# Order of GpSimd's back substitution and of its decay transfers, and place of the decay exponentials on ScalarE, in a block of attention and gated DeltaNet

## The reference

```python
gcum = jnp.cumsum(g, axis=-1)
decay = jnp.exp(jnp.where(causal, gcum[..., :, None] - gcum[..., None, :], -jnp.inf))
a_mat = jnp.einsum('bnhid,bnhjd->bnhij', k_beta, k) * decay * strict
rhs = jnp.concatenate([v * beta[..., None], k_beta * jnp.exp(gcum)[..., None]], axis=-1)
sol = lax.linalg.triangular_solve(eye + a_mat, rhs, left_side=True, lower=True,
                                  unit_diagonal=True)
qk = jnp.einsum('bnhid,bnhjd->bnhij', q, k) * decay
```

## Time and profile before

| | |
|---|---|
| median of 3 runs | 1907.46 us (1907.27 to 1907.67) |
| the profiled execution | 1907.71 us, of which the span is 1905.9 us |
| TensorE busy | 1887.0 us, 99% of the span |
| VectorE busy | 1250.8 us, 66% |
| ScalarE busy | 1039.5 us, 55% |
| GpSimd busy | 105.6 us, 6% |
| granted TensorE clock | 0.998 |

### The profile page before, as it was taken

One profiled execution on the slowest core, in us unless ns is written; L12 is line 12 of the kernel. 1 busy time (PEld: TensorE's weight loads), 2 busy tenths in 40 slices (PEclk: granted clock), 3 DMA queues, 4 the chain that ended last, 5 costly groups with the idle time before them and its releaser, 6 DMA issues.

```text
span 1905.9 us, 27743 instructions
## 1 busy us (share of the span) xinstructions
PE 1887.0 (99%) x9497; PEld 1585.5 (83%) x9497; DVE 1250.8 (66%) x2189; ACT 1039.5 (55%) x2108; POOL 105.6 (6%) x208
## 2 busy tenths in 40 slices
PE   9999999999999999999999999999999999999997
PEld 8888888888888888888888788888888888888886
DVE  6658888898888665655666776555555555545555
ACT  4447776667767554555444655544444445444442
POOL 2001022111220100000000000000000000000000
PEclk9999999999999999999999999999999999999999
DMA  8666565555654657665565465556555555665552
GB/s 318 208 157 179 149 146 138 116 165 130 151 132 142 193 189 248 198 199 190 195 245 181 152 219 199 190 185 197 181 194 189 186 183 191 224 207 189 196 199 89
DMA packets 204180, 349.63 MB, mean 183 GB/s; under 512 B 6768, under 2 KB 73024, under 8 KB 203088
## 3 DMA queue, kind: packets, MB, share of 16 engines
q1 hardware_dynamic: 200704, 334.00, 52.7%
q0 software_dynamic: 3264, 14.47, 5.6%
q10 hardware_dynamic: 144, 0.26, 0.0%
HBM read 344.32 MB, written 2.10 MB: 182 GB/s over the span
## 4 chain that ended last, share of the span: by engine, by line
PE 83%; DVE 9%; issue 4%; POOL 2%; ACT 2%; DMA 1%; DVEq 1%; ACTq 0%; POOLq 0%; SPq 0%
PE dense L658 23%; PE dense L660 23%; PE dense L659 23%; PE dense L646 5%; PE dense L648 3%; DVE lo L1518 2%; DMA raw<-in_w_in_dram 1%; POOL less L571 1%; POOL sub L574 1%; PE chain L822 1%; PE chain L1104 1%; DVE pad L1689 0%; DVE qd L1814 0%; PE chain L924 0%; PE chain L916 0%
## 5 line engine op out<-in xcount | busy, mean ns | idle before, releaser
L1518 DVE TENSOR_TENSOR lo<-raw,hi 128x512 fp32r<-128x512 f32 x1252 | 843.0, 691 | 427.2 <-ACT hi L1154 423.8
L1154 ACT ACTIVATE hi<-raw 128x512 fp32r<-128x512 f32 x1252 | 777.0, 630 | 632.3 <-PE dense L660 611.5
L658 PE MATMUL dense<-hi,xs 128*128 128x512 f32 x1376 | 540.0, 392 | 1.8 <-DVE xs L2081 1.1
L660 PE MATMUL dense<-lo,xs 128*128 128x512 f32 x1376 | 536.2, 390 | 0.0
L659 PE MATMUL dense<-hi,xs 128*128 128x512 f32 x1376 | 535.9, 389 | 0.0
L646 PE MATMUL dense<-xs,hi 128*128 128x512 f32 x1024 | 379.9, 410 | 0.0
L658 PEld LDWEIGHTS dense<-hi,xs 128*128 128x128 f32 x1376 | 258.4, 188 | 55.8 <-DVE xs L2081 2.0
L660 PEld LDWEIGHTS dense<-lo,xs 128*128 128x128 f32 x1376 | 258.4, 188 | 53.9
L659 PEld LDWEIGHTS dense<-hi,xs 128*128 128x128 f32 x1376 | 258.5, 188 | 52.4
L648 PE MATMUL dense<-xs,lo 128*128 128x256 f32 x1024 | 286.3, 280 | 0.0
L646 PEld LDWEIGHTS dense<-xs,hi 128*128 128x128 f32 x1024 | 192.5, 188 | 42.9 <-DVE lo L1518 3.1
(11 more groups left out here) (327 smaller groups left out, 1435.7 us busy)
## 6 DMA issues: line engine op xcount, KB each, us to landing
raw<-in_w_in_dram SPq DMA_DIRECT2D x115, 1024.0 KB, 5.1
raw<-in_w_ffn_gate_dram SPq DMA_DIRECT2D x44, 1024.0 KB, 5.1
raw<-in_w_ffn_up_dram SPq DMA_DIRECT2D x44, 1024.0 KB, 5.1
raw<-in_w_ffn_down_dram SPq DMA_DIRECT2D x44, 1024.0 KB, 5.0
raw<-in_w_br_att_dram SPq DMA_DIRECT2D x16, 1024.0 KB, 5.1
raw<-in_w_br_dn_dram SPq DMA_DIRECT2D x16, 1024.0 KB, 5.0
raw<-in_w_out_dram SPq DMA_DIRECT2D x16, 1024.0 KB, 5.1
raw<-in_w_ple_gate_dram SPq DMA_DIRECT2D x16, 1024.0 KB, 5.0
```

What stands on the lines that cost most here:

```text
L658: pe.matmul(o, ah, hi[:, s, :], start=(k == 0), stop=False)
L660: mm = pe.matmul(o, ah, lo[:, s, :], start=False, stop=(k == nk - 1))
L1154: act.activation(parts(pos, n)[0], raw[:, slot, off:off + 512], ACT.Copy).then_inc(sem("hi_ready"), 1)
L1518: dve.tensor_tensor(wl, raw[:, slot, off:off + 512], wh.bitcast(F32), ALU.subtract).then_inc(sem("lo_ready"), 1)
```

## The change

Three things move, and no instruction is added or taken away.

1. On GpSimd `back_rows(p)` stands ahead of the two waits and the two transfers of the next pair (`decay_in(p + 1)`), where it stood behind them.
2. On ScalarE the copy into `blk` stands ahead of the copy of `ck` into `k1` (L1279), both after quarter 2. In the last pair's chain, outside the loop, their order stays.
3. On ScalarE the four exponentials of `Em` come after quarter 26 of the turn, where they came after quarter 12.

```diff
@@ gpsimd
             for p in range(PAIRS):
                 power_of("length", "k_eps", row[:, 1, :], row[:, 4, :], p)
+                back_rows(p)
                 if p + 1 < PAIRS:
                     pool.wait_ge(sem("egb"), p + 1)
                     pool.wait_ge(sem("am"), p + 1)
                     decay_in(p + 1)
-                back_rows(p)
-                if p + 1 < PAIRS:
                     causal(p + 1)
                     unit_blocks(p + 1)
                     power_of("rms", "o_eps", row[:, 8, :], row[:, 9, :], p)
@@ scalar
             def qk_front(k, i):
 
-                if k == 12:
+                if k == 26:
                     act.wait_ge(sem("am"), i + 1)
                     for x in range(4):
...
+            def rows_copy(p):
+
+                act.wait_ge(sem("x_prod"), nth("x_prod", 0, p))
+                act.activation(blk[:].rearrange("p x i j -> p (x i j)"), C[:, 0, 0:256], ACT.Copy).then_inc(sem("vu_out"), 1)
+
             def inverse_k(k, p):
 
-                if k == 5:
-                    act.wait_ge(sem("x_prod"), nth("x_prod", 0, p))
-                    act.activation(blk[:].rearrange("p x i j -> p (x i j)"), C[:, 0, 0:256],
-                                   ACT.Copy).then_inc(sem("vu_out"), 1)
-                elif k in (9, 11, 13):
+                if k in (9, 11, 13):
...
                 for k in range(32):
                     split(pos, k)
                     if chain:
+                        if copy_at(k) == 5:
+                            rows_copy(i - 1)
                         chain_k(stage_at(k), i - 1)
```

More of the change, by code:

```diff
@@ L1405, in _ @@
                     chain_k(stage_at(LAST_AT[n]), PAIRS - 1)
+                    if copy_at(LAST_AT[n]) == 5:
+                        rows_copy(PAIRS - 1)
                     inverse_k(copy_at(LAST_AT[n]), PAIRS - 1)
```

## The result

The changed kernel takes 1913.27 us (median of 8 runs, 1912.81 to 1914.15), the kernel before 1907.72 us (8 runs beside them). The ratio is 1.0029, with a 95% interval of 1.0019 to 1.0039: 5.55 us slower, where 3.85 was forecast. The time lies inside the range, 2.0 us above the predicted value and 0.3 us above the forecast's own case (1909.2 to 1913). By the prediction's bound of 1911.3 it counts as slower, to which it gave 0.38, and not as no change, to which it gave 0.52; its own value lay on that bound.

A forecast was written before the change was run, and what follows sets the result against it. TensorE, at 99% of the span, was taken as the bound. The substitution and exponentials together cost 0.7 us and the mask addition 3.15, so 3.85 us slower: 1911.3 us, range 1904.5 to 1915.

The forecast's parts named there:

- the forecast's own case: Whole kernel: the case holding the predicted value, 1909.2 to 1913 us, chance 0.48.
- the prediction's bound of 1911.3: Whole kernel: time above which it counts as slower; a difference under 0.2% (3.8 us) counts as no change.
- What bounds the kernel: TensorE, at 99% of the span; it loses 0.60 us a turn at L822 and 0.40 at L842.
- Part 3: ScalarE's later exponentials delay a weight copy, so VectorE's `lo` and `AT` come 0.4 us late; L782 held 0.10 to 0.15.
- Parts 1 and 2: GpSimd's substitution ahead of L822 starts 0.6 us early, ends 0.3 early: 1.8 us gained by themselves.
- The transfers' lateness: GpSimd's later transfers also move the next weight transfer; costed at nothing, covered by VectorE being 5 quarters ahead.
- The mask addition: GpSimd's addition lands beside VectorE's transposes and delays the next `lo`, so L842: 0.45 us a turn, 3.15 us slower.
- The sum: Whole kernel: 0.7 us plus 3.15 us, so 3.85 us slower, median 1911.3 us.
- The early start: Rival, chance 0.13: substitution not held to VectorE's stream, L822's 0.60 us stall goes, 3.6 us gained, 1903.9 us.
- The third rival: The mask addition holds VectorE in full, transposes too: 1.1 us a turn at L842, 1915.9 us, from 1913; chance 0.14.

The follow-up runs named there:

- e8: e6 with VectorE's masking of `Yz` put ahead of the scaling of attention's `sE`: 1902.78 us.
- e1: The kernel before with only the exponentials of `Em` moved, from after quarter 12 to after quarter 26: 1910.56 us.
- e3: The changed kernel with GpSimd's mask addition moved behind its copy of unit blocks, transfers left as changed: 1907.48 us.
- e4: The changed kernel with the exponentials after quarter 22 and GpSimd's mask addition behind its copy of unit blocks: 1904.73 us.
- e6: e4 with GpSimd's copy of the unit rows into `sub` put ahead of its wait for `blk`: 1902.52 us.
- e7: The kernel before with the exponentials after quarter 22 and the mask addition behind the copy of unit blocks: 1906.74 us.
- e5: The changed kernel with the exponentials back after quarter 12: 1910.29 us.

## Why the prediction was right, and where its sizes were off

**What bounds the kernel** held. All of the loss is in steps of TensorE at three products of the chain. One number there was wrong: 0.40 us a turn was called lost at L842, by the usual step of 0.12. The usual step into its 64-column products is 0.21 (e8), so 0.31 was lost before: 2.2 us in 7 turns and not 2.8.

**Part 3** held in its mechanism. By starts the `lo` came 0.44 us late (turn 3: 362.37 - 361.54 = 0.83, where the step behind the same kind of operation is 0.39), of which the row shows 0.34 as idle; 0.4 was forecast, and part 3 alone does it too (e1). The size at L782 was too small: 0.10 to 0.15 us was forecast, 0.36 measured, 0.28 of it at the start and 0.08 inside the group. The prediction counted the whole 0.28 between ScalarE's start on `AT` and L782 as slack. After, L781 follows that start by 0.12 (368.64 - 368.52), so the slack was 0.16, and 0.44 - 0.16 = 0.28.

**Parts 1 and 2** held. `blk` ends at 373.96 and the copy starts at 374.02. Five steps beside the run of `lo` are slow where four were (0.57 to 0.67), and one step of the quick kind was gained. For all that comes of the three parts up to L821 the forecast was 0.1 us a turn; measured, 0.36 lost at L781 less 0.18 won at L821 is 0.18, and over the six turns the net is 1.0 us instead of 0.7. That the stall at L821 would stay near 0.6 was wrong for the same reason: it fell to 0.42, because the hold moved to L781. The two errors nearly cancel in the sum, since what is lost at L781 is not lost again at L821.

**The transfers' lateness** at nothing was right (e3), but its cover, the 5 quarters that VectorE is ahead, was not drawn on, since the new order made no weight transfer slow. The two of turn 4 that were issued behind GpSimd's transfers before (at 372.83 and 375.40) took 12.3 and 12.4 us to land; in the changed kernel they are issued ahead of GpSimd's (at 375.06 and 377.67) and took 5.1 and 5.3, and the next one, behind them, took 5.6. No `hi` in the loop waited for a transfer in either kernel, so the faster landing won nothing either.

**The mask addition** is the term that was mis-sized. Its place was right, at the late end: forecast 10.4 to 10.7 us behind the start of L821 (389.6 or 389.9, less 379.17), measured 391.88 - 381.16 = 10.72, with the lead of 0.27 ahead of the issue that the forecast allowed for. It lies beside the transposes at L1769, and these took 0.62 us as before. By the Trainium skill, GPSIMD Engine Reference, § 1 Specifications, contention comes with a VectorE instruction that has two SBUF inputs or a 2-port mode; the trace agrees, with 0.62 unchanged for the one kind and 1.53 for the other. No run here changes the inputs of either operation, so that it is these inputs which decide rests on that page and on these two kinds of rows. The `lo` behind them began 0.98 us ahead of the addition's end (391.88 + 1.29 - 392.19) and lost 0.85 of it; the difference is the 0.1 that the forecast had taken off. Because L1818 was free, VectorE stood at the transposes 0.20 us earlier than before (10.38 us behind L821, before 10.58), which leaves 0.65 at the operation behind the `lo`, and 0.68 at TensorE. The prediction's working gave 0.4 to 0.7 for this, and then took 0.45, near its low end, for fear of a landing so late that the addition would miss the `lo`. The landing was not late: 10.13 us, before 10.15. Over the seven turns the step into L841 lost 4.5 us in place of 3.15. Taking the addition away gives more (e3: 5.8), since L841 then also keeps the 0.15 us a turn that the free L1818 wins against the kernel before.

**The sum**, with what was measured over all turns: 1.0 + 4.5 = 5.5, against 5.34 in the loop and 5.55 in all. Of the rivals, none came about as described. The early start won 1.2 us of its 3.6 in the changed kernel and 1.8 with the exponentials at quarter 22 (e4); the whole 3.6 was won only when the copy went ahead too (e6), and there as well the steps inside VectorE's stream came at one for each `lo`. The third rival's case begins at 1913, and the time lies there, but not by its mechanism: the addition did not hold the transposes, and it held VectorE for 0.85 us and not for 1.1.

## What to carry to other kernels

Before a GpSimd operation is moved, look at what VectorE has at the new place, and how far that place is from the next product that waits for VectorE; here taking the same addition away gained 5.8 us at one place (e3) and 1.2 at another (e7), and it cost nothing at a third, where VectorE waits for ScalarE on both sides (e4). Of a change in several parts run each alone: this one held a gain of 2 us under a loss of 3 from a move that was not needed (e5) and a loss of 4.5 from one that could be turned aside (e3), and with both mended and one free copy taken off the path (e6) it beats the kernel before by 0.28%. When an order is full, a stall removed at one product can come up at the next (e8): look for the next product that hangs on the same engine's order.

## What was not expected of the hardware

GpSimd's operations of 28 to 20 columns keep pace with VectorE's subtractions when they lie beside them: one for each `lo`, 0.56 to 0.67 us, and 0.24 to 0.27 when VectorE is not in such a run. VectorE's run takes 3.30 us for five `lo` with five such steps beside it (changed kernel, turn 4) and 3.27 with four (before). With a wide GpSimd operation it is the other way round: the addition of 512 columns took 1.29 us beside a held `lo`, and 1.67 beside the held L1814 before, and VectorE lost 0.85 and 1.1 us. In these rows the short operations of GpSimd took as long as if they waited for VectorE, and VectorE lost time to the long one.
